# Wider opening tiles, early output products in other places, and routing on unscaled logits in a one-core decoder layer

## What is computed

```
h = _rmsnorm(x, norm_mix_g)
proj = h @ w_in
...
x = x + concatenate([y_a, y_b], -1) @ w_out
hf = _rmsnorm(x, norm_ffn_g)
logits_c = hf @ router_coarse;  p_c = softmax(logits_c);  grp = argmax(logits_c)
lf = (hf @ router_fine)[grp];   p_f = softmax(lf);        top_p, top_i = top_k(p_f, 2)
gates = p_c[grp] * top_p / sum(top_p)
x = x + sum over the two experts of gates * ((silu(hf @ w_gate[e]) * (hf @ w_up[e])) @ w_down[e])
y = _rmsnorm(x, norm_final_g)
```

## Time and profile before

| | |
|---|---|
| median of 3 runs | 2088.92 us (2087.84 to 2090.7) |
| the profiled execution, time and span | 2090.2 us, 2088.0 us |
| PE busy, PE weight load | 1718.4 us (82%), 1018.3 us (49%) |
| DVE, ACT, POOL busy | 605.0, 282.0, 124.0 us |
| chain that ended last | PE 54%, DMA 26%, DVE 12% |
| HBM read | 499.87 MB |

### The profile page before, as it was taken

One profiled execution on the slowest core, in us unless ns is written; L12 is line 12 of the kernel. 1 busy time (PEld: TensorE's weight loads), 2 busy tenths in 40 slices (PEclk: granted clock), 3 DMA queues, 4 the chain that ended last, 5 costly groups with the idle time before them and its releaser, 6 DMA issues.

```text
span 2088.0 us, 26301 instructions
## 1 busy us (share of the span) xinstructions
PE 1718.4 (82%) x9068; PEld 1018.3 (49%) x9068; DVE 605.0 (29%) x1113; ACT 282.0 (14%) x550; POOL 124.0 (6%) x101
## 2 busy tenths in 40 slices
PE   7998999999899989898979767676768768686663
PEld 4776767677677767676754322222322223132111
DVE  6636263545444454521011102011111101011012
ACT  2221212222121212111131000000000000000001
POOL 0201111110202020200000000000000000000000
PEclk9999999999999999999988889798988979798777
DMA  7223222322132222227136999999999999999992
GB/s 264 106 75 109 75 88 75 108 74 89 64 105 77 73 106 81 82 115 263 48 154 282 421 421 421 421 422 421 422 422 422 422 422 422 422 422 422 422 421 100
DMA packets 91181, 510.60 MB, mean 245 GB/s; under 512 B 23424, under 2 KB 26624, under 8 KB 31776
## 3 DMA queue, kind: packets, MB, share of 16 engines
q1 hardware_dynamic: 91056, 509.61, 61.2%
q0 software_dynamic: 48, 0.12, 0.0%
HBM read 499.87 MB, written 9.82 MB: 244 GB/s over the span
## 4 chain that ended last, share of the span: by engine, by line
PE 54%; DMA 26%; DVE 12%; issue 3%; ACT 1%; SPq 1%; DVEq 1%; ACTq 0%
DMA arena<-w_up 15%; PE ps_PJ L576 15%; DVE arena L1199 12%; PE ps_C L885 8%; DMA arena<-w_gate 8%; PE ps_PJ L774 7%; PE ps_PJ L856 4%; DMA arena<-w_down 3%; PE ps_PJ L863 2%; PE ps_C L634 2%; PE ps_C L657 1%; ACT arena L953 1%; SPq L490 1%; PE ps_SB L917 1%; PE ps_C L917 1%
## 5 line engine op out<-in xcount | busy, mean ns | idle before, releaser
L576 PE MATMUL ps_PJ<-arena 128*128 128x320 f32 x1792 | 542.2, 434 | 4.0 <-ACTq L355 4.0
L885 PE MATMUL ps_C<-arena 128*32 128x512 f32 x2048 | 304.6, 750 | 151.8 <-DMA arena<-w_up 117.4
L576 PEld LDWEIGHTS ps_PJ<-arena 128*128 128x128 f32 x1792 | 319.8, 190 | 111.5 <-issue 11.1
L885 PEld LDWEIGHTS ps_C<-arena 128*32 128x32 f32 x2048 | 80.1, 133 | 370.7 <-issue 366.1
L1199 DVE TENSOR_TENSOR arena<-ps_PJ,arena 128x512 f32<-128x512 f32 x32 | 22.1, 692 | 658.1 <-PE ps_PJ L856 658.1
L953 ACT ACTIVATE arena<-ps_C 128x512 f32<-128x512 f32 (+1 forms) x68 | 46.2, 679 | 1121.4 <-PE ps_C L885 603.6
L1653 POOL TENSOR_TENSOR arena<-arena 128x640 f32<-128x640 f32 (+2 forms) x80 | 118.2, 1477 | 787.5 <-DVEq L355 429.4
L1199 DVE TENSOR_TENSOR arena<-arena 128x320 f32<-128x320 f32 (+11 forms) x242 | 150.9, 624 | 37.2 <-ACTq L355 16.4
L1199 DVE TENSOR_TENSOR arena<-arena,ps_PJ 128x512 f32<-128x512 f32 (+2 forms) x112 | 73.6, 657 | 290.9 <-PE ps_PJ L863 166.8
L774 PE MATMUL ps_PJ<-arena 128*128 128x320 f32 x512 | 144.9, 437 | 4.8 <-DVEq L355 4.8
L856 PE MATMUL ps_PJ<-arena 128*128 128x128 f32 (+1 forms) x768 | 140.6, 313 | 0.4 <-DVEq L355 0.4
(11 more groups left out here) (174 smaller groups left out, 1356.5 us busy)
## 6 DMA issues: line engine op xcount, KB each, us to landing
arena<-w_gate SPq DMA_DIRECT2D x128, 1024.0 KB, 19.0
arena<-w_up SPq DMA_DIRECT2D x128, 1024.0 KB, 18.9
arena<-w_down SPq DMA_DIRECT2D x128, 1024.0 KB, 18.9
arena<-win SPq DMA_DIRECT2D x59, 1024.0 KB, 4.9
arena<-w_out SPq DMA_DIRECT2D x16, 1024.0 KB, 8.6
arena<-xT SPq DMA_DIRECT2D x8, 640.0 KB, 6.1
arena<-s_ret SPq DMA_DIRECT2D x8, 512.0 KB, 4.1
o_sret<-arena SPq DMA_DIRECT2D x8, 512.0 KB, 3.9
```

Source lines behind the costliest of these rows:

```text
L576: last = mm(pj(j)[:, 0:T], wt[j % NSLOT][:, kt, :], hT[:, kt, :], start=kt == 0, stop=kt == KT - 1)
L885: last = mm((GB, UB)[u][h * CAP:(h + 1) * CAP, :], xg[:, kt, h * CAP:(h + 1) * CAP], w[h][:, k, :], start=kt == 0, stop=kt == KT - 1)
```

## The change

Three parts, none of which changes what is computed.

**Opening.** SP issues tile 0 after the first `xT` piece. ScalarE squares blocks in groups of 2, 2, 4, 4, 4 (`SETUP`) into three wide buffers; VectorE multiplies and adds whole groups (a broadcast gain, so tensor_tensor in place of tensor_scalar), and folds four blocks' sum to one at the end. The product with `ones` stands after the first of the four groups. `normalise` works on four blocks at a time, all four groups before `lpart`.

```
-                if i == 1:
+                if i == 0:
                     piece(0, 0)
...
+            for i, (k0, n_k) in enumerate(SETUP):
+                dve.wait_ge(sq_done, i + 1)
+                h = hT[:, k0:k0 + n_k, :]
+                TT(h, h, gm[:, k0:k0 + n_k, None].broadcast_to([P, n_k, T]), ALU.mult).then_inc(sem("scaled"), 1)
+                if k0 >= 4:
+                    TT(squares[0], squares[0], squares_of(k0, 4).rearrange("p k n -> p (k n)"), ALU.add).then_inc(sq_used, 1)
+            TT(squares[0][:, 0:2 * T], squares[0][:, 0:2 * T], squares[0][:, 2 * T:4 * T], ALU.add)
+            last = TT(t1, squares[0][:, 0:T], squares[0][:, T:2 * T], ALU.add)
...
-            normalise(range(8))
-            dve.wait_ge(used, NL)
+            for g in range(4):
+                normalise(g)
             TT(lpart, psum["C2"][:, 0:T], bsv, ALU.mult).then_inc(sem("lora_part"), 1)
-            normalise(range(8, KT))
```

```
-                        for _ in range(2 if it[1][0] in "aresm" else 1):
-                            if early:
-                                out_proj(*early.pop(0))
+                        for _ in range({"s3": 2, "mu": 4, "va": 5}.get(it[1], 1)):
+                            out_proj(*early.pop(0))
```

```
-            dve.wait_ge(named["root_done"], 1)
-            RECIP(rstd, rstd)
             dve.wait_ge(named["lg_full"], 1)
-            for t, (t0, nt) in enumerate(TT_):
-                TSC(lg[0:nt, t, :], LB[0:nt, t * 64:t * 64 + 36], rstd[0:nt, t:t + 1], None, ALU.mult)
+            CP(lg[:, 0:2, :], LB[:, 0:128].rearrange("p (t n) -> p t n", t=2)[:, :, 0:36])
+            CP(lg[0:HD, 2, :], LB[0:HD, 128:164])
...
+            TT(e2, m2, m1, ALU.subtract)
+            dve.wait_ge(named["root_done"], 1)
+            RECIP(rstd, rstd)
+            TT(q4[:, :, :], q4[:, :, :], wide(rstd, NG), ALU.mult).then_inc(named["cmax_done"], 1)
+            TT(e2, e2, rstd, ALU.mult).then_inc(named["dm_done"], 1)
...
                 select(sel0, 0)
                 if first(rd):
+                    k0 = n[1]
+                    gates()
                     rounds_needed()
```

## The result

The changed kernel takes 2076.36 us, median of 4 runs (2074.06 to 2077.08), against 2089.77 us of the kernel before (2087.84 to 2090.70, 4 runs). The ratio is 0.9936, 95% interval 0.9923 to 0.9949: 13.4 us faster, within 10.7 and 16.1. The forecast was 2074.5 in 2071 to 2079; sign and range held. It was 1.9 us too low. One of its three terms was 1.0 too large, and a gain that no term has paid for a part of losses that no term has either. The profiled execution took 2077.03; the spans of the two profiled executions are 2088.0 and 2075.2, so 12.8 are to be accounted for.

A forecast was written before the change was run, and what follows sets the result against it. Bound: TensorE until about 1085 us, then the expert weights' stream, so the end follows its first load. Terms -5.9 opening, -4.4 closing, -4.1 router sum to -14.4: 2074.5 us for the median, range 2071 to 2079.

The forecast's parts named there:

- What bounds it: Whole kernel: the end is the first expert-weight load behind the gap, at 1111.97 us, plus a constant.
- It doesn't pass through: Rival, 3%: something other than the gate product sets the stream's restart, so all gain is lost, 2089 us.
- Opening, tile 0: Opening: tile 0 ends at 21.5 instead of 25.67 us, so TensorE gains 4.2.
- the slower rival: Opening: wide tensor_tensor costs 3.2 ns a column, 4.1 us per 1280-column operation, total 2097.5 us; chance 2%.
- the half-clock end of the range: Opening: tile 0's four last products at half clock cost 1.2 to 2.1 us, leaving a gain of 3.8.
- Opening, VectorE: Opening: VectorE reaches `lora_raw` 7.6 us sooner, the TensorE wait at 57.28 goes, 5.9 us sooner in all.
- That chain is what TensorE waited for, 1.72 us: Opening: lora shifts, k's shift and ScalarE's square were said to cause TensorE's 1.72 us wait at 57.28.
- would have waited until 49.7: Opening: with VectorE 7.6 us sooner TensorE's wait would end at 49.7, but TensorE arrives at 51.4.
- Closing: Behind the loop: early products dealt out anew bring s3 5.7 us sooner and the x load 4.4 sooner.
- Router: Router: expert picks start before ScalarE's squares are done, saving 4.1 us, ends 3.6 and 4.4.
- No wait, or a few hundredths: Router: VectorE's sum of squares, eleventh operation of the picks, would hardly wait for its input at 1085.61.
- the rival of 2067: Router: a 6.2 us wait keeps TensorE's clock up through the gather and gate products, 7 to 8 us less; 4% with its smaller form in range.

The follow-up runs named there:

- the last version: Changed kernel with six and one idle products, first tile's ScalarE square ahead of the tanh, VectorE's gates and weighted selection behind the first batch's gathered blocks: 2068.64 us, 0.9895.
- The idle products alone: Changed kernel with seven unread fp32 products on TensorE, six in its wait for the experts' choice, one behind the ranking's totals: 2071.14 us, 0.9911.
- the kernel with the closing alone: Kernel before the change with only the early products dealt out anew: 2087.46 us, ratio 0.9986.
- the padded kernel: Changed kernel with 68 empty instructions ahead of the opening on VectorE alone: 2075.65 us, one execution.
- the one padded on both engines: Changed kernel with 68 empty instructions on VectorE and 36 on ScalarE ahead of the opening: 2075.80 us, one execution.
- the opening kernel: Kernel before the change with only the opening part edited: 2084.20 us, ratio 0.9975.

## Why the prediction was right, and where it was not

**What bounds it: right.** The first load moved by 13.4, the stream behind it took 929.63 instead of 929.90. "It doesn't pass through" is out.

**Opening, tile 0: right,** 4.56 gained for 4.2. Ten operations of 1280 columns took 1.49 us each, as drawn from the rows of 320 and 512 columns; the slower rival needed 3.2. Four narrow gains would have saved nothing: one took 0.39 before, four so 1.56. That rival's 2.04 for 640 columns belongs to operations beside GpSimd's: the two of 640 columns at the start of the changed kernel, with GpSimd idle, took 1.80 together, 0.83 each and a gap. By the Trainium skill ("SBUF — State Buffer", section "Who interferes with whom") the two engines share a port pair and block each other only where they overlap; the trace agrees, with 0.83 and 2.04. TensorE pauses 0.83 and 0.86 between tile 0's groups, and the four blocks behind each pause ran at 0.54 a block all the same, so the half-clock end of the range stayed away.

**Opening, VectorE: the failed step** is "That chain is what TensorE waited for, 1.72 us" and with it "would have waited until 49.7". VectorE's 7.6 were 8.1. But a wait is put down to one releaser, ScalarE's square, and I took what fed the square for its cause. ScalarE before, tanh of za and k's square:

```profile
55.60 0.53 ACT L953 ACTIVATE arena<-ps_SB,arena 128x320 f32<-128x320 f32 x1 [1.09 <-PE ps_SB L594]
56.53 0.56 ACT L953 ACTIVATE arena<-arena 128x320 f32<-128x320 f32 x1 [0.41 <-DVEq L355]
```

The square started 0.41 behind the tanh. In the changed kernel, where k is there long before, 0.12 lie between them all the same, so 0.29 was VectorE's, and the rest of the wait was TensorE's own product of za through ScalarE. TensorE reached that product 4.64 sooner (50.22 for 54.86), which with 0.29 makes the 4.93 that came of the 5.9. ScalarE's queue was missing from the rows I read.

**Not in the prediction:** the loop's 1.6 us. I had written of the loops as unchanged, and their work is.

**Closing: right.** Against the shift at `us` (6.52), u1's and u2's operations on VectorE come 4.85 and 5.59 sooner (forecast 4.8 and 5.7), s3 5.58 (5.7); the new wait at u2 is 0.60 (0.8), and the one behind va 2.12 (2.1). The x load comes 4.76 sooner, not 4.4. The term that was mis-sized is what six products cost between s3 and va, 0.90 for 1.35: s3 to va was 4.28 and is 5.18. The wait ahead of mu was 0.51, as I took it:

```profile
936.29 0.81 PE L709 MATMUL ps_C<-arena 128*128 128x320 f32 x2 [0.51 <-ACTq L355]
```

But a product ahead of a wait shows its full length, mu 0.81, where the next one follows after 0.54 if there is no wait; the last product of s3, ahead of mu's wait, showed 0.39 for 0.23. Two waits hid two such ends, 0.43 together, and I had counted the waits alone.

**Router: right,** 3.83 of 4.1. Nine operations stand ahead of the sum of squares, not ten, and took 2.03 us, so VectorE was there at 1075.41 and waited 0.51; the squares were ready 3.9 behind the logits in both kernels. "No wait, or a few hundredths" was half a microsecond off. It came in part from a sum: ten at 0.2 to 0.25 from 1083.2 end at 1085.2 to 1085.7, not at "1085.6 to 1086", and so allowed a wait of up to 0.4.

**The clock: the rival of 2067 stayed out, as forecast,** but the length of the wait, my reason, did not decide it. In the changed kernel the granted clock was at 0.50 from 1074 on, some 1.1 us into the 6.45 of waiting, and in the last version it fell at the same place with idle products already running. They brought it back: ranking, gather, and gate product to first load took 2.74 + 7.56 + 6.46 in the changed kernel and 1.42 + 4.30 + 3.66 in the last version, 7.4 less. So the rival's price of 7 to 8 was right and its condition, that a shorter wait keeps the clock, false. The idle products alone gave 2071.1; 2068.6 took two more edits. The Trainium skill ("TensorE: Matmul & The Clock Gate", Part 1) has idleness take the clock and sustained work give it back; the runs agree. What I had not priced are the places behind. Table by stretch of the changed kernel around the x load (columns as in the earlier trace rows):

```profile
932.00:938.00 6.00, 3.87 (x10) 2.26 (x11) 2.40 (x6) 0.00 (x0) 0.00 (x0) 0.66 0.75 248
938.00:940.50 2.50, 2.50 (x8) 1.68 (x7) 0.20 (x1) 0.00 (x0) 0.00 (x0) 0.50 1.01 418
940.50:945.00 4.50, 4.50 (x18) 3.19 (x17) 0.00 (x0) 0.00 (x0) 0.00 (x0) 0.97 0.76 93
```

And of the kernel with the closing alone, which comes to the same place 6.5 us later:

```profile
939.00:944.00 5.00, 3.88 (x8) 2.02 (x8) 1.56 (x5) 0.00 (x0) 0.00 (x0) 0.66 0.79 245
944.00:950.00 6.00, 5.80 (x24) 4.22 (x25) 0.57 (x2) 0.00 (x0) 0.00 (x0) 1.00 1.07 288
```

The same work at 0.50 until 940.5, and back at 1.00 from 944: x load to logits 139.40 and 137.91. What sets the moment at which the clock comes back was not found. It is not the change's order of work, since the padded kernel with its loop 1.6 us later, otherwise the same, has 137.94 (the one padded on both engines, 139.54). From the transposition on this stretch cost the profiled execution of after 1.55 against the one of before. With 0.30 more behind the gate product and 0.85 more behind the last piece (0.70 of it in the products on that piece, 0.12 in the last combination) it lost 2.7 us, which I put down to the clock.

**The sum.** Forecast 5.9 + 4.4 + 4.1 = 14.4. Measured 4.93 + 4.79 + 3.92 = 13.64 in the three places (start to `ss`; `us` to the transposition; logits to gate), 1.59 in the loop, 0.27 in the stream, less 2.70 for the clock: 12.80, the difference of the spans. That the forecast landed so near is in part luck: a gain that it didn't know, 1.59, paid for more than half of the losses that it didn't know, 2.70.

## What to carry to other kernels

A wait's releaser names the last link, not its cause: before crediting a faster engine with a wait, read the queue of the engine in between, and see what stands ahead of the releasing instruction and what that waits for. When the work that ends a gap runs at half clock behind a long wait, try to fill the wait with just as many idle products as fit, counted from their measured length (six gained here, thirteen and nine did not); what was hidden under the slow work must then be moved too. And before the period of a loop is credited to an edit, shift the loop with empty instructions and measure again.

## What the runs showed of the hardware

- A loop's place in VectorE's instruction stream changed its period from 110.94 to 110.68 us, by one gap of 0.59 or 0.22 ahead of one operation: at 269 instructions 0.59, with padding to 269 again 0.59, at 201 and at 329 0.22.
- An fp32 product of 512 columns takes 0.86 us at full clock, as two records of 0.43; six took 5.42, and 7.11 where the clock fell to 0.50 under them.
- A VectorE tensor_tensor on 1280 fp32 columns takes 1.493 us with GpSimd idle. One on 640 takes 0.83 with GpSimd idle and 2.04 beside GpSimd's own.
- Executions of the opening kernel, and of the closing kernel, fall into two groups some 3.5 and 5 us apart, the slower with a mean granted clock of 0.913 to 0.918, the faster with 0.924 to 0.930. In the profiled ones of the changed and the closing kernel the last combination's 24 records take 13.51 and 11.94.
